# Output projection, second norm and router logits in one stage of a two-block network on one Trainium2 core

## The reference

```python
def rmsnorm(x, g):
    xf = x.astype(jnp.float32)
    y = xf * lax.rsqrt(jnp.mean(xf * xf, axis=-1, keepdims=True) + EPS)
    return (y * g.astype(jnp.float32)).astype(x.dtype)
...
        mix = jnp.concatenate([rmsnorm(y_hy, hy_norm_g[l]).astype(x.dtype), y_hg.astype(x.dtype)], axis=-1) @ w_out[l]
        x = x + g1 * mix
...
        h2 = modulate(rmsnorm(x, norm2_g[l]), sh2, sc2)
        x = x + g2 * ec_moe(h2, router_w[l], exp_w1[l], exp_w3[l], exp_w2[l])
...
    return rmsnorm(x, final_g)
...
    aff = jax.nn.softmax(jnp.einsum('bnd,de->bne', h, router_w).astype(jnp.float32), axis=-1)
    gates, idx = lax.top_k(jnp.swapaxes(aff, 1, 2), cap)
...
    shift, scale, gate = jnp.split(jax.nn.silu(c) @ w_mod + b_mod, 3, axis=-1)
    shift_c, scale_c, gate_c = jnp.split(jax.nn.silu(c_ctx) @ w_mod + b_mod, 3, axis=-1)
    h = rms_norm(x, norm_g) * (1 + scale[:, None]) + shift[:, None]
```

## Time and profile before

| | us |
|---|---|
| median of 3 runs | 4401.6 |
| profiled execution | 4406.15 |
| span of its trace | 4404.4 |
| TensorE busy in the span | 3838.6 (87%) |
| VectorE | 2558.8 (58%) |
| ScalarE | 1913.1 (43%) |
| GpSimd | 698.3 (16%) |

### The profile page before, as it was taken

One profiled execution on the slowest core, in us unless ns is written; L12 is line 12 of the kernel. 1 busy time (PEld: TensorE's weight loads), 2 busy tenths in 40 slices (PEclk: granted clock), 3 DMA queues, 4 the chain that ended last, 5 costly groups with the idle time before them and its releaser, 6 DMA issues. The chain is left out here.

```text
span 4404.4 us, 44390 instructions
## 1 busy us (share of the span) xinstructions
PE 3838.6 (87%) x17507; PEld 2917.0 (66%) x17507; DVE 2558.8 (58%) x2731; ACT 1913.1 (43%) x2509; POOL 698.3 (16%) x582
## 2 busy tenths in 40 slices
PE   7899787894677789999999999799888897997988
PEld 2788643334675328877787777678767576786766
DVE  6421265326985468888888888652166524523753
ACT  4411110005545227677767677533166314423641
POOL 0200023210002100212111120320022223201222
PEclk9999898996888889999999999899999898999999
DMA  6322314101104569999999999534141234434123
GB/s 245 131 92 100 113 48 178 45 31 70 36 15 168 195 231 372 363 373 369 372 369 373 373 369 371 168 114 134 70 154 42 98 115 148 116 115 178 57 73 119
DMA packets 391941, 782.21 MB, mean 178 GB/s; under 512 B 26070, under 2 KB 109153, under 8 KB 391346
## 3 DMA queue, kind: packets, MB, share of 16 engines
q1 hardware_dynamic: 375350, 727.72, 46.2%
q0 software_dynamic: 11456, 41.16, 2.9%
q10 hardware_dynamic: 4928, 10.49, 0.7%
HBM read 667.80 MB, written 111.51 MB: 177 GB/s over the span
## 5 line engine op out<-in xcount | busy, mean ns | idle before, releaser
L2553 DVE TENSOR_TENSOR moe_w_low<-moe_w_raw,moe_w_high 128x2048 fp32r<-128x2048 f32 x384 | 882.1, 2342 | 164.4 <-ACT moe_w_high L2506 163.3
L2506 ACT ACTIVATE moe_w_high<-moe_w_raw 128x2048 fp32r<-128x2048 f32 x384 | 715.2, 1913 | 302.2 <-DMA moe_w_raw<-in_exp_w 293.8
L172 PE MATMUL moe_bank<-moe_w_high,moe_xgT_high 128*128 128x512 f32 x1024 | 404.0, 395 | 16.9 <-DVE moe_w_low L2553 12.0
L174 PE MATMUL moe_bank<-moe_w_high,moe_xgT_low 128*128 128x512 f32 x1024 | 399.6, 390 | 0.0
L173 PE MATMUL moe_bank<-moe_w_low,moe_xgT_high 128*128 128x512 f32 x1024 | 399.3, 390 | 0.0
L2775 DVE TENSOR_REDUCE layer_att_nb<-layer_att_scores 128x1 f32<-128x1280 f32 (+1 forms) x144 | 197.1, 1369 | 139.0 <-PE layer_att_scores L2681 139.0
L172 PEld LDWEIGHTS moe_bank<-moe_w_high,moe_xgT_high 128*128 128x128 f32 x1024 | 192.7, 188 | 63.0 <-DVE moe_w_low L2553 15.0
L172 PE MATMUL layer_front_bank<-layer_front_w_high,layer_front_hT_high 128*128 128x512 f32 (+1 forms) x608 | 230.1, 378 | 0.0
L174 PE MATMUL layer_front_bank<-layer_front_w_high,layer_front_hT_low 128*128 128x512 f32 (+1 forms) x608 | 223.7, 368 | 0.0
L173 PE MATMUL layer_front_bank<-layer_front_w_low,layer_front_hT_high 128*128 128x512 f32 (+1 forms) x608 | 223.5, 368 | 0.0
L174 PEld LDWEIGHTS moe_bank<-moe_w_high,moe_xgT_low 128*128 128x128 f32 x1024 | 192.6, 188 | 40.8
(11 more groups left out here) (488 smaller groups left out, 8286.4 us busy)
## 6 DMA issues: line engine op xcount, KB each, us to landing
moe_w_raw<-in_exp_w SPq DMA_DIRECT2D x192, 2048.0 KB, 10.3
mods_raw<-in_ada_w SPq DMA_DIRECT2D x12, 2048.0 KB, 9.2
h_raw<-in_w_mod SPq DMA_DIRECT2D x12, 2048.0 KB, 8.1
front_raw<-in_w_in SPq DMA_DIRECT2D x32, 512.0 KB, 6.3
proj_t<-front_out SPq DMA_DIRECT2D x48, 256.0 KB, 2.0
moe_w_raw<-in_w_in SPq DMA_DIRECT2D x24, 512.0 KB, 6.5
layer_front_raw<-in_w_in SPq DMA_DIRECT2D x24, 512.0 KB, 6.2
k_high<-layer_front_stageda SPq DMA_DIRECT2D x20, 512.0 KB, 3.3
```

Of the source, the lines that this page charges most:

```text
L172: nc.tensor.matmul(out, lhs[0], rhs[0], start=start, stop=False)
L174: return nc.tensor.matmul(out, lhs[1], rhs[0], start=False, stop=stop)
L2506: nc.scalar.activation(hi, x, ACT.Copy).then_inc(high, 1)
L2553: nc.vector.tensor_tensor(lo, x, hi.bitcast(F32), ALU.subtract).then_inc(low, 1)
```

## The change

The output projection, the second norm and the logits become one stage, `stage_mix_norm`. In it each tile of `x1` stays in on-chip memory: it is squared, scaled, turned and modulated there, and TensorE multiplies it by the router's matrix as soon as `hT` has the tile (8 products of 128 by 16), straight into the form that the softmax reads. `x1` and `xn2` are still stored. The weights and tiles lie in the buffers of the expert weights. The output halves have two pairs of banks instead of three, and the turned heads one bank instead of two.

The 12 groups of vectors lose their bias product, their turns, their placing and the four scale vectors. Only rows without bias are stored. Groups 0 to 3 move to the recurrence: their weights come in 16 pieces of 512 KB through 7 slots in a buffer that is not used yet; TensorE takes 12 pieces ahead of its first turn and 4 behind the first states. Groups 4 to 11 are loaded, computed and stored in the router stage: 6 groups ahead of the turn of the ranks, and one product for each expert in the picks. Each layer's projection reads its 48 rows of 128 back, adds the bias, turns them with one transpose and makes the scales; each layer's output projection adds the bias to its two gates.

In layer 0's projection the transposes of the rescaled tiles stand behind the job of their round instead of ahead of it.

```diff
+LATE = [(l, g) for l in range(2) for g in range(6)]
+LATE_EARLY = 4
...
+def late_product(core, out, raw, k):
+    return core.nc.tensor.matmul(out, core.silu[:, 16 + k:16 + k + 9:8], raw, start=(k == 0), stop=(k == KD - 1))
...
-            self.nc.tensor.matmul(b, self.ones[:, :], self.bias[:, i * BANK:(i + 1) * BANK], start=True, stop=False)
-    def columns(self, pe, i):
-        pe.wait_ge(self.copied, i + 1)
-        if i:
-            pe.wait_ge(self.placed, i)
-        for s in range(4):
-            last = self.nc.tensor.transpose(self.bank[2][:, 2 * s:2 * s + 2], self.rows[i % self.ROWS][:, s * P:(s + 1) * P],
-                                            self.core.ident[0:2, 0:2])
-        last.then_inc(self.turned, 1)
...
-def stage_norm(core, name, segs, hT, xn_dram, late, hosted):
...
+                if late is not None:
+                    sp.dma_start(mod_row[:, :], core.mod_rows[1 + late].rearrange("v (c p) -> (v c) p", p=P)).then_inc(mod_loaded, 16)
+                    for v in range(2):
+                        sp.dma_start(mod_bias[24 * v:24 * v + 24, :], io["b_mod_2"][late].rearrange("(c p) -> c p", p=P)
+                                     ).then_inc(mod_loaded, 16)
...
-                    if 0 <= i + 2 < n:
+                    if 0 <= i + 2 < FIRST:
                         turn(i + 2)
+                    if i == -2 and late is not None:
+                        pe.wait_ge(mod_whole, 1)
+                        nc.tensor.transpose(bank[3][:, 0:48], mod_row[:, :], core.ident[0:48, 0:48]).then_inc(mod_turned, 1)
...
+                    if rescaled_tile(i + 2):
+                        turn(i + 2)
...
+                def mod_columns():
+                    dve.wait_ge(mod_loaded, 48)
+                    nc.vector.tensor_tensor(mod_row[:, :], mod_row[:, :], mod_bias[:, :], ALU.add).then_inc(mod_whole, 1)
+                    dve.wait_ge(mod_turned, 1)
+                    step(nc.vector.tensor_copy(cols[:, :, :], bank[3][:, 0:48].rearrange("p (v c) -> p c v", v=2)))
+                    for v in range(2):
+                        g = AT_A["norm_g_2"] + 8 * late
+                        ready_ = nc.vector.scalar_tensor_tensor(core.sc[3 + 2 * late + v][:, :], cols[:, 8:16, v], 1.0,
+                                                                core.col_a[:, g:g + 8], ALU.add, ALU.mult)
+                        if v == 0:
+                            step(ready_)
+                    ready_.then_inc(mod_ready, 1)
+                    dve.wait_ge(mod_ready, 1)
...
+    NLP, LSLOTS, LATE_AHEAD = 4 * LATE_EARLY, 7, 12
...
+                def late_pair(q):
+                    if q >= LSLOTS:
+                        sp.wait_ge(late_used, q - LSLOTS + 1)
+                    i, k = divmod(2 * q, KD)
+                    sp.dma_start(spare[:, 2 * (q % LSLOTS):2 * (q % LSLOTS) + 2, :], late_weights(core, i, k, k + 2)
+                                 ).then_inc(core.load[4 + q % LSLOTS].sem, 16)
...
+                for q in range(LSLOTS, NLP):
+                    late_pair(q)
...
+                for i in range(LATE_EARLY):
+                    act.wait_ge(late_done, i + 1)
+                    nc.scalar.activation(late_row[0:2, i * BANK:(i + 1) * BANK], bank[i][0:2, :], ACT.Copy).then_inc(late_copied, 1)
...
+                def late_pairs(q0, q1):
+                    for q in range(q0, q1):
+                        i, k = divmod(2 * q, KD)
+                        pe.wait_ge(core.load[4 + q % LSLOTS].sem, core.load[4 + q % LSLOTS].at(q // LSLOTS + 1))
+                        for c in range(2):
+                            last = late_product(core, bank[i][0:2, :], spare[:, 2 * (q % LSLOTS) + c, :], k + c)
+                        if k + 2 == KD:
+                            last.then_inc(late_done, 1)
+                            pe.wait_ge(late_done, i + 1)
+                            pe.sem_inc(late_used, 1)
+                        else:
+                            last.then_inc(late_used, 1)
+                late_pairs(0, LATE_AHEAD)
                 pe.wait_ge(inputs, 32)
...
+                late_pairs(LATE_AHEAD, NLP)
+                pe.wait_ge(late_copied, LATE_EARLY)
...
-def stage_mix_out(core, name="mixout"):
+def stage_mix_norm(core, raw, yo, hT, logits, name="mixout"):
...
+                    if t >= RX:
+                        sp.wait_ge(xturned, 2 * (t - RX) + 2)
+                        sp.wait_ge(core.store[4 + t % RX].sem, core.store[4 + t % RX].at(t // RX))
...
+                def measure(t):
+                    act.wait_ge(added, 2 * t + 2)
+                    core.act(act, nc.scalar.activation(junk, x1[t % RX], ACT.Square, accum_out=xss[:, t:t + 1]))
+                    nc.scalar.activation(xrms[:, t:t + 1], xss[:, t:t + 1], ACT.Sqrt, bias=core.eps[:, 0:1],
+                                         scale=1.0 / D).then_inc(xrooted, 1)
+
+                def modulate(t):
+                    act.wait_ge(xturned, 2 * t + 1)
+                    for k in range(4):
+                        last = nc.scalar.activation(hT[:, k, t * P:(t + 1) * P], bank[5][:, k * P:(k + 1) * P],
+                                                    ACT.Identity, bias=sh[:, k:k + 1], scale=sc[:, k:k + 1])
+                    last.then_inc(out_a, 1)
+
...
-                for t in range(1, NT):
+                for t in range(NT + 2):
+                    if t >= 2:
+                        modulate(t - 2)
                     if t + 1 < NT:
-                    place(t)
+                        place(t + 1)
+                    if 1 <= t <= NT:
+                        measure(t - 1)
+                    if t + 2 < NT:
+                        head(t + 2)
...
+                def turn_x(t):
+                    pe.wait_ge(xnormed, t + 1)
+                    if t >= 1:
+                        pe.wait_ge(out_a, t)
+                        pe.wait_ge(out_v, t)
+                    for half in range(2):
+                        for k in range(4):
+                            c = (4 * half + k) * P
+                            last = nc.tensor.transpose(bank[5 + half][:, k * P:(k + 1) * P], x[t % RX][:, c:c + P],
+                                                       core.ident[:, :])
+                        last.then_inc(xturned, 1)
+
+                def route(t):
+                    if t == 0:
+                        pe.wait_ge(routing, 16)
+                    pe.wait_ge(out_a, t + 1)
+                    pe.wait_ge(out_v, t + 1)
+                    for k in range(KD):
+                        last = nc.tensor.matmul(logits[:, t * E:(t + 1) * E], hT[:, k, t * P:(t + 1) * P], rw[:, k, :],
+                                                start=(k == 0), stop=(k == KD - 1))
+                    last.then_inc(routed, 1)
 
...
-                        if n >= 3:
-                            pe.wait_ge(added, n - 2)
+                        if n >= 2:
+                            pe.wait_ge(added, n - 1)
...
+                    if t:
+                        turn_x(t - 1)
+                    if t >= 2:
+                        route(t - 2)
+                route(NT - 2)
+                turn_x(NT - 1)
+                route(NT - 1)
...
+                def normalise(t):
+                    dve.wait_ge(xrooted, t + 1)
+                    step(nc.vector.reciprocal(xrms[:, t:t + 1], xrms[:, t:t + 1]))
+                    dve.wait_ge(added, 2 * t + 2)
...
-                for t in range(NT):
+                for t in range(NT + 2):
+                    if t >= 2:
+                        modulate(t - 2)
+                    if 1 <= t <= NT:
+                        normalise(t - 1)
                     if t + 2 < NT:
                         gated_output(t + 2)
-                    results(t)
+                    if t < NT:
+                        results(t)
 
...
-        IN_TOPK = late.N - 3
+        NL = late.N - LATE_EARLY
+        IN_TOPK = NL - 2
...
-                for i in range(hosted, IN_TOPK):
+                for i in range(IN_TOPK):
                     late.products(pe, i)
-                    if i > hosted:
-                        late.columns(pe, i - 1)
-                late.columns(pe, IN_TOPK - 1)
...
-                    for c in range(3 * e // 2, 3 * (e + 1) // 2):
-                        i, k = divmod(c, KD)
-                        late.products(pe, IN_TOPK + i, k, k + 1)
-                        if i and k == 2:
-                            late.columns(pe, IN_TOPK + i - 1)
-                late.columns(pe, late.N - 1)
+                    i, k = divmod(e, KD)
+                    late.products(pe, IN_TOPK + i, k, k + 1)
...
+                sp.dma_start(gate_bias[:, :], io["b_mod_2"][l, 2 * D:3 * D].partition_broadcast(P)).then_inc(gates, 16)
...
-                dve.wait_ge(gates, 32)
+                dve.wait_ge(gates, 48)
+                for v in range(2):
+                    core.dve(dve, nc.vector.tensor_tensor(gate[v], gate[v], gate_bias[:, :], ALU.add))
```

370 lines of the change are left out of this document (134 added, 236 removed).

## The result

The changed kernel takes 4341.5 us (median of 4 runs, 4339.8 to 4349.2) against 4404.5 before (4 runs), a ratio of 0.986 with a 95% interval of 0.984 to 0.988. In a second comparison, later, it was 4342.7 (5 runs) against 4405.8 (9 runs), 0.985 (0.984 to 0.986). Both times 63 us went. The forecast was 4334, 67 less, in a range of 4314 to 4358.

The account below looks back on a forecast made before the run. TensorE bounds the output projection; behind it the reload with its norm, then the vectors' groups. −82.6 + 15.7 + 2.6 − 5.5 + 2.6 = −67.2 from 4401.6 gave 4334 us, range 4314 to 4358.

Parts of the forecast that it names:

- Term A: Last addition of the output projection to the experts: 92.4 us instead of 175.0, so −82.6.
- tail: From the last addition to the router's first reduction, over norm, modulation, logits and stage change: 11.5 us.
- twice the turns at the low clock: Price of the last tile's logits, taken as double the 1.97 us of eight transposes: 3.8 us (1.9 to 7.6).
- Term B: Joint stage's tiles: added transposes and logits raise the period from 11.34 to 14.2 us, +15.7 in all.
- The chain: VectorE and ScalarE work per tile in the joint stage: 13.3 us, 0.9 to spare within 14.2.
- The rival that GpSimd holds VectorE up: Joint stage: gating beside GpSimd's pass makes a tile 15.6 us, +8 to +11, total about 4343; chance 0.15.
- Term C: Recurrence: 12 pieces free ahead of the first turn, last eight products exceed idle time; +2.6 us (0 to +12).
- second rival: Recurrence: the vectors' pieces make turn, states or loads up to 12 us late, total about 4344; chance 0.13.
- Term D: Front of layer 0: first job 4.8 us earlier, then GpSimd's tables hold job 5; −5.5 us (−11 to +3).
- Term E: Front of layer 1: three DMA issues 1.2 us and columns about 1.4; +2.6 us (0 to +5).
- sign of being wrong: Layer 1: being late by more than 5 us was listed as showing the forecast wrong.
- slower rival: Joint stage: TensorE stays at 1.2 GHz, tiles up to 28.4 us, total about 4455; chance 0.03.

Follow-up runs that it names:

- a_again: The changed kernel profiled once more with no edit; 4337.1 us.
- early2: Changed kernel with two groups of vectors instead of four in the recurrence and ten in the router; 4355.2 us.
- best: Changed kernel with GpSimd's tables in three parts and the router's first group of weights loaded during the joint stage; 4335.2 us against 4342.7.
- route_end: Changed kernel with the logits of all eight tiles behind the last tile's turn instead of one tile each round; 4351.4 us.
- b_again: The kernel before the change profiled once more with no edit; 4405.6 us.
- tables_split: Changed kernel with GpSimd's tables made in three parts behind the low parts of three tiles instead of in one piece; 4335.2 us.
- turns_old: Changed kernel with the projections' old order of turns, each turn ahead of the job of its round; 4346.0 us.
- ahead16: Changed kernel with all 16 pieces of the vectors' weights ahead of the recurrence's first turn instead of 12; 4341.9 us.
- ahead8: Changed kernel with 8 pieces ahead of the recurrence's first turn and 8 behind the first states; 4343.0 us.

## Why the prediction was right

**Term A, forecast −82.6.** Measured −82.1 in the first profiles and −83.1 in the means of all (175.3 to 92.1). The steps hold one by one: tail 11.0 to 12.5 (11.5), slots 55.0 (54.7), picks 21.9 (21.6), experts 3.5 behind (4.6). Why the tail has two values the timelines tell, first profile after:

```profile
1472.70 3.56 PE L2085 MATMUL h_bank<-mixout_rw,h_hT 128*128 128x16 f32 x16 [1.82 <-DVE h_hT L2153]
1476.10 1.95 PE L2075 MATMUL mixout_bank<-ident,moe_w_raw 128*128 128x128 f32 x8
```

and a_again:

```profile
1469.71 2.12 PE L2085 MATMUL h_bank<-mixout_rw,h_hT 128*128 128x16 f32 x16 [1.82 <-DVE h_hT L2153]
```

The same 16 records after the same 1.82 us of idle time take 3.56 or 2.12, as the clock falls. That is also the worth of "twice the turns at the low clock", 3.8 in the sum. early2 shows that the groups cost what the sum gives them, and the last of the six ends 54.4 us after the first reduction, where the sum had 54. One reading was off without harm: the search ends 51.8 us after that reduction and not 50.6, since the softmax ahead of it waits longer for ScalarE and for TensorE's turn (0.97 and 2.07 us instead of 0.53 and 1.23). With the groups gone from its path, this would be the limit, as best shows.

**Term B, forecast +15.7.** From the first addition to the last it was 85.1 and is 100.2: +15.1. The period was put at 14.2 and is 13.1 to 14.0. The chain, put at 13.3, is 13.1 by route_end. The rival that GpSimd holds VectorE up falls: all eight gatings take 0.69. Here the rule of the Trainium skill ("SBUF — State Buffer", section "SBUF: two separate sides") agrees with the 2.97 of before, and with their absence where the two passes no longer meet: GpSimd's passes now fall into VectorE's wait for the root (it idles 2.40 us up to 1420.29, and GpSimd's pass from 1417.69 takes 2.39). In the kernel before the two met once the other way round, VectorE first by a little; its row and GpSimd's:

```profile
1418.74 0.69 DVE L2126 TENSOR_TENSOR mixout_og<-mixout_og,mixout_g 128x512 f32<-128x512 f32 x1
1418.77 2.92 POOL L2161 TENSOR_TENSOR mixout_y_low<-mixout_yT,mixout_y_high 128x1024 fp32r<-128x1024 f32 x1
```

VectorE kept its 0.69 there, and it was GpSimd's pass that took longer, 2.92 instead of 2.40.

**Term C, forecast +2.6.** Measured +0.3. The term was mis-sized by 2.3. The first profiles alone would have seemed to confirm it, since TensorE's later rows stand 3.2 us later there; but ScalarE enters the stage 2.9 later already, and b_again, the kernel before, does so by 2.7. The 12 pieces did push the first turn back, by 5 us within the stage (1046.58 − 1015.04 against 1038.63 − 1012.15), which the sum had denied: its loads did not keep up.

```profile
hgrn_r<-in_w_mod SPq DMA_DIRECT2D x16, 512.0 KB, 10.9
```

A piece took 10.9 us in the median from issue to landing, where the sum had a quarter of 8.1, about 2. The wait of 10.45 us is over the 10 that the prediction named as the sign of its second rival; the sign came, its cost did not. VectorE's own list is the reason. It has no idle time ahead of its copy of the first state, neither before nor after:

```profile
1046.03 0.28 DVE L1903 COPY hgrn_s<-hgrn_bank 128x128 f32<-128x128 f32 x1
```

```profile
1049.09 0.29 DVE L1842 COPY hgrn_s<-hgrn_bank 128x128 f32<-128x128 f32 x1
```

That is 33.88 and 34.05 us into the stage, so the states are no later although TensorE's first turn is. The four pieces behind them ran at the full clock (7.03, where the sum took 9); the products after them stand 50.6 us into the stage instead of 49.4, and of that 1.2 the stage's end keeps 0.3.

**Term D, forecast −5.5.** Measured −0.9. This step failed. The first job does start 4.9 earlier, as forecast, and job 5 waits for GpSimd. But it starts at 2765.78 − 2714.83 = 51.0 behind the first turn, where the sum had 2829.7 − 2781.7 = 48.0. The sum left GpSimd's tables where they stood, 35.2 behind the first turn (2816.93 − 2781.70). They start at 38.1, 2.8 later:

```profile
2746.78 1.04 PE L810 MATMUL layer_front_bank<-ident,moe_w_raw 128*128 128x128 f32 x8
```

```profile
2752.89 1.99 POOL L640 MEMSET layer_front_stagedb<- 128x1024 f32 x2
```

The tables follow the low part of the tile turned here. The new order puts that turn behind the job of its round, 32.0 behind the first turn instead of 29.1 (2810.82 − 2781.70), and low part and tables move back with it. So the edit that brought the first job forward pushed back what job 5 waits for; that the tables hold job 5 is shown by tables_split. Job 5 is then only 2.1 earlier than before (53.1, 2834.76 − 2781.70), and at the end of the front the means keep 0.9; where the rest goes no run separates. In all the new order gave 3.6 where the sum had 7.0, and what was added cost 2.7 where it had 1.5 (turns_old). (The sum's 2825.9 for job 5 is a slip as well: 2792.8 and five times 6.36 make 2824.6. Nothing hung on it, since GpSimd came later.)

**Term E, forecast +2.6.** Measured +0.7 for layer 1's front. The loads and columns cost less than the sum had; which of the two was put too high no run shows.

**What is in no term.** Attention and mixing: −3.2 in layer 0 and +6.5 in layer 1, at other granted clocks with the same instructions. With the experts and the output projections, which only gained the gates' bias, it comes to +2.2. Here too a sign of being wrong came without its cause: layer 1 was later by more than 5 us, through the clock and not through its front. The errors of the terms are −0.8 (A and B, by the table), −2.3 (C), +4.6 (D) and −1.9 (E), −0.4 together. From −67.2 that leads to −65.4; the mean spans differ by 65.2 (4404.1 to 4338.9), the medians by 63. So the sum was right because its large terms, A and B, were, and their steps are shown one by one. That the total came within 4 us is also luck: the small terms cancelled, C, D and E were off by most of their size, and nothing in the prediction foresaw the untouched stages. The slower rival fell: the clock was 1.00 in the middle of the joint stage.

## What to carry to other kernels

A stage that only reloads, norms and turns what the stage before had on chip is worth nearly its whole length if the work fits beside an engine's bound: 83 us went for 15 us of longer tiles. Before a difference of some microseconds in one stage is put down to a change, look at several profiles, stage by stage: here the experts alone differ by 6 within one kernel, and by 12 over all kernels with the same code there (1143.0 in turns_old to 1155.0). Work that fills a gap must stand in that gap; the same pieces ahead of it (ahead16) cost 2.8 and beyond it (ahead8) 6.4.

## What was not expected of the hardware

Untouched stages changed by −3 and +6.5 us, with the same instructions and another granted clock of TensorE (0.94 to 0.95 and 0.97 or 0.96 to 0.94 in the windows), alike in all three profiles of the changed kernel. Neither is fixed: turns_old, which contains the change, has 331.8 us in layer 0 at 0.94, as before it, and tables_split 288.9 in layer 1 at 0.96. In this kernel such stages are a source of some 6 us either way that no sum over its own edits contains.
